# Per-engine instruction orders from a readiness planner in two attentions

## The reference

```python
s_s = jnp.einsum('bgrqd,bgqkd->bgrqk', qb, ks).astype(jnp.float32) - slopes * d_s
p_s = _masked_softmax(s_s, d_s >= 0)
o_s = jnp.einsum('bgrqk,bgqkd->bgrqd', p_s.astype(vs.dtype), vs)
...
kv = (_rmsnorm(c_kv, kv_norm) @ w_ukv).reshape(B, S, H, MLA_NOPE + MLA_V)
k_nope, v = kv[..., :MLA_NOPE], kv[..., MLA_NOPE:]
s = (jnp.einsum('bqhd,bkhd->bhqk', qn, k_nope)
     + jnp.einsum('bqhd,bkd->bhqk', qr, k_rope)).astype(jnp.float32)
p = _masked_softmax(s, kpos[None, :] <= tq[:, None])
return jnp.einsum('bhqk,bkhd->bqhd', p.astype(v.dtype), v)
```

## Time and profile before

| | |
|---|---|
| median of 3 runs | 1872.5 us (1850.19 to 1872.74) |
| profiled execution | 1867.99 us, its span 1866.4 us |
| PE matmul busy | 1539.8 us, 83% of the span |
| PE weight loads | 1231.9 us, 66% |
| DVE / ACT / POOL busy | 766.0 / 635.1 / 487.1 us |
| mean granted clock of PE | 0.887 |

### The profile page before, as it was taken

The page is one execution under the profiler, slowest core; times in us unless marked ns, Lnnn a source line. Parts: engine busy times, 40 slices in busy tenths (PEclk is TensorE's granted clock), DMA queues, the critical chain, the costliest instruction groups (busy, mean ns, idle before and its releaser), DMA issues. The chain is left out here.

```text
span 1866.4 us, 21535 instructions
## 1 busy us (share of the span) xinstructions
PE 1539.8 (83%) x8024; PEld 1231.9 (66%) x8024; DVE 766.0 (41%) x1416; ACT 635.1 (34%) x1402; POOL 487.1 (26%) x455
## 2 busy tenths in 40 slices
PE   8999997886647777877598799768889888988596
PEld 6888885554535565656477588646777777766475
DVE  2110012443565666666435000245555455555443
ACT  3112212431125556555211122225454444445200
POOL 2222221001023222221234322132243323340235
PEclk9999997656758899999799799869999999999798
DMA  5111310112031000000532222010000000000422
GB/s 169 46 51 57 123 34 21 34 34 74 1 66 40 17 18 18 18 12 1 182 102 91 74 90 83 17 54 15 15 1 15 15 15 10 6 1 1 182 102 102
DMA packets 38790, 93.51 MB, mean 50 GB/s; under 512 B 5137, under 2 KB 9250, under 8 KB 37922
## 3 DMA queue, kind: packets, MB, share of 16 engines
q1 hardware_dynamic: 38690, 92.16, 15.6%
HBM read 68.03 MB, written 18.87 MB: 47 GB/s over the span
## 5 line engine op out<-in xcount | busy, mean ns | idle before, releaser
L1092 ACT ACTIVATE mla_probs_t_hi<-mla_ps_turned 128x512 fp32r<-128x512 f32 x192 | 91.7, 490 | 156.7 <-PE mla_ps_turned L1050 155.9
L1110 DVE TENSOR_TENSOR mla_probs_t_lo<-mla_ps_turned,mla_probs_t_hi 128x512 fp32r<-128x512 f32 x192 | 105.0, 554 | 86.5 <-ACT mla_probs_t_hi L1092 85.1
L1110 DVE TENSOR_TENSOR nsa_probs_t_lo<-nsa_ps_turned,nsa_probs_t_hi 128x512 fp32r<-128x512 f32 (+1 forms) x192 | 98.7, 521 | 76.2 <-ACT nsa_probs_t_hi L1092 75.1
L237 POOL TENSOR_TENSOR l0p_w_lo<-l0p_w_raw,l0p_w_hi 128x512 fp32r<-128x512 f32 (+1 forms) x56 | 68.6, 1225 | 216.3 <-ACT l0p_w_hi L221 216.3
L1084 ACT ACTIVATE nsap_probs<-nsa_ps_scores,nsa_neg_max 128x640 f32<-128x640 f32 (+7 forms) x128 | 89.6, 700 | 71.0 <-DVE nsa_neg_max L1104 64.3
L1092 ACT ACTIVATE nsa_probs_t_hi<-nsa_ps_turned 128x512 fp32r<-128x512 f32 (+1 forms) x192 | 84.1, 461 | 82.0 <-PE nsa_ps_turned L1050 81.3
L1104 DVE TENSOR_REDUCE mla_neg_max<-mla_ps_scores 128x1 f32<-128x512 f32 (+7 forms) x128 | 96.7, 756 | 34.9 <-PE mla_ps_scores L1919 34.6
L1084 ACT ACTIVATE base_region<-mla_ps_scores,mla_neg_max 128x512 f32<-128x512 f32 (+7 forms) x128 | 94.9, 741 | 46.9 <-DVE mla_neg_max L1104 40.3
L221 ACT ACTIVATE l0p_w_hi<-l0p_w_raw 128x512 fp32r<-128x512 f32 (+1 forms) x56 | 34.0, 606 | 225.0 <-PE l0p_ps_acc L64 203.3
L1104 DVE TENSOR_REDUCE nsa_neg_max<-nsa_ps_scores 128x1 f32<-128x640 f32 (+7 forms) x128 | 90.1, 704 | 38.7 <-PE nsa_ps_scores L1303 37.8
L62 PE MATMUL out_ps_y<-out_w_hi,out_o_t_hi 128*128 128x512 f32 x256 | 104.0, 406 | 0.1
(11 more groups left out here) (255 smaller groups left out, 3941.8 us busy)
## 6 DMA issues: line engine op xcount, KB each, us to landing
l0p_w_raw<-in_w_dram SPq DMA_DIRECT2D x48, 256.0 KB, 2.7
out_w_raw<-in_w_out_dram SPq DMA_DIRECT2D x16, 512.0 KB, 4.4
l1p_w_raw<-in_w_dram SPq DMA_DIRECT2D x24, 256.0 KB, 3.1
mla_w_raw<-in_w_heads_dram SPq DMA_DIRECT2D x8, 640.0 KB, 3.8
l0p_x_raw<-in_x_t_dram SPq DMA_DIRECT2D x8, 512.0 KB, 3.4
silu_gates_scratch<-l0p_silu_out SPq DMA_DIRECT2D x16, 256.0 KB, 2.1
out_res<-in_x_dram SPq DMA_DIRECT2D x8, 512.0 KB, 5.0
x_scratch<-out_w_raw SPq DMA_DIRECT2D x8, 512.0 KB, 2.9
```

The source lines that it names most:

```text
L237: nc.gpsimd.tensor_tensor(wl[:, k % WR, 0:w], raw[:, k % RAW, 0:w], wh[:, k % WR, 0:w].bitcast(F32), ALU.subtract).then_inc(lo_ready, 1)
L1092: self.nc.scalar.activation(self.pth[:, m % N_SPLIT, c], self.p_t[f.turn_slot[m] % N_TURN][:, c], ACT.Copy).then_inc(self.hi_done, 1)
L1110: self.nc.vector.tensor_tensor(self.ptl[:, m % N_SPLIT, c], self.p_t[f.turn_slot[m] % N_TURN][:, c], self.pth[:, m % N_SPLIT, c].bitcast(F ...
```

## The change

`Flow` goes. `Plan` takes lanes: lists of tasks for one engine or a choice of engines, each task with a cost and the tasks that it needs. It repeatedly places, at the earliest possible start, the head of a lane that was ready first, and keeps an order for each engine alone. A finished task counts as seen by others REACH later (PE 200 ns, ACT and DVE 45, POOL 80). Values, backs, turns, and rows with units are four lanes of PE; evictions may go to ACT or DVE in both attentions. Turn banks are given out in the order in which turns and backs are placed.

`packed` puts several narrow key blocks of a step into one turn bank, up to four tiles: a step of the first half has 3 packs instead of 4 key blocks, one of the second half 7 instead of 8 (causal) or 5 instead of 8 (window). A pack has one `hi` and one `lo`; its transposes and value matmuls are as many as before. A turn waits for the last row that it reads, no longer for the last of the step.

In MLA the values of two pairs are projected together in even pairs, 24 matmuls of 256 columns per half, into a ring of V_SLOTS = 3 pair slots. Weight blocks are 1536 columns for even pairs, of which odd pairs load and split only 1024. All units of the next pair now alternate with the last rows of a pair; in the first pair the first row stands behind one q and one k unit. POOL waits for the previous pair's last rows before it overwrites q and k. The cost functions of the planner are `matmul_cost` max(107, 5 + 0.45 n), `act_cost` 165 + 0.845 n, `exp_cost` 455 + 0.84 n, `dve_cost` 150 + 1.055 n (ns, n columns).

```diff
+class Plan:
+
+
+
+
+    REACH = {"PE": 200, "ACT": 45, "DVE": 45, "POOL": 80, "SP": 0}
+
+    def __init__(self, n_turn):
+        self.n_turn = n_turn
+        self.lanes, self.done, self.order = [], {}, {e: [] for e in self.REACH}
+        self.slot, self.slots, self.drains = {}, [], []
+
+    def lane(self, engines, tasks, takes_slot=False):
+        self.lanes.append((engines, list(tasks), takes_slot))
+
+    def drain_lane(self, engine, drain_of):
+
+        self.lanes.append(((engine,), self.drains, False))
+        self.drain_of = drain_of
+
+    def _ready(self, tasks, takes_slot):
+        key, cost, needs = tasks[0]
+        times = [self.done.get(k) for k in needs]
+        if takes_slot and len(self.slots) >= self.n_turn:
+            times.append(self.done.get(self.drain_of(self.slots[-self.n_turn])[0]))
+        return None if None in times else max(times, default=0)
+
+    def run(self):
+        free = dict.fromkeys(self.REACH, 0)
+        while True:
+            best = None
+            for e in free:
+                heads = []
+                for n, (engines, tasks, takes_slot) in enumerate(self.lanes):
+                    if e in engines and tasks:
+                        ready = self._ready(tasks, takes_slot)
+                        if ready is not None:
+                            heads.append((ready, n))
+                if heads:
+                    ready, n = min(heads)
+                    start = max(ready, free[e])
+                    if best is None or start < best[0]:
+                        best = (start, e, n)
+            if best is None:
+                break
+            start, e, n = best
+            engines, tasks, takes_slot = self.lanes[n]
+            key, cost, needs = tasks.pop(0)
+            free[e] = start + cost
+            self.done[key] = start + cost + self.REACH[e]
+            self.order[e].append(key)
+            if takes_slot:
+                self.slot[key] = len(self.slots)
+                self.slots.append(key)
+                self.drains.append(self.drain_of(key))
+        assert not any(tasks for _, tasks, _ in self.lanes)
...
+def packed(groups):
+
+    left, packs = list(groups), []
+    while left:
+        pack = [left.pop(0)]
+        for g in sorted(left, key=lambda g: -len(g[1])):
+            if sum(len(tiles) for b, tiles in pack) + len(g[1]) <= 4:
+                pack.append(g)
+                left.remove(g)
+        packs.append(pack)
+    return packs
...
+    def seen_by(self, m):
+
+        s, pack = self.packs[m]
+        tiles = {i for b, ts in pack for i in ts}
+        return max(k for k in range(self.first_row[s], self.last_row(s) + 1) if self.steps[s]["rows"][self.rows[k][1]][0] in tiles)
...
+        plan.lane(("PE",), [(("values", m), 30 + sum(2 * matmul_cost(len(tiles) * P) for b, tiles in self.packs[m][1]),
+                             [("lo", m)] + value_needs(self.packs[m][0])
+                             + [("evict", s - 1) for s in steps if s and m == self.first_pack[s]]) for m in packs])
+        plan.lane(("PE",), [(("back", s), 428, [("evict", s)]) for s in steps], takes_slot=True)
+        plan.lane(("PE",), [(("turn", m), 107 * self.pack_cols(m) // P, [("exp", self.seen_by(m))]) for m in packs], takes_slot=True)
+        plan.lane(("PE",), main)
+        plan.lane(("ACT",), [(("exp", k), exp_cost(self.row_cols(k)), [("max", k)]
+                              + [("turn", self.last_pack(s - 2)) for s in [self.rows[k][0]] if s >= 2]
+                              + [("totals", s - 4) for s in [self.rows[k][0]] if s >= 4]) for k in range(len(self.rows))])
+        plan.lane(("ACT",), [(("hi", m), act_cost(self.pack_cols(m)), [("turn", m)] + [("values", m - N_SPLIT)] * (m >= N_SPLIT))
+                             for m in packs])
+        plan.lane(("DVE",), [(("max", k), dve_cost(self.row_cols(k)), [("row", k)]) for k in range(len(self.rows))])
+        plan.drain_lane("DVE", lambda key: (("lo", key[1]), dve_cost(self.pack_cols(key[1])), [("hi", key[1])])
+                        if key[0] == "turn" else
+                        (("totals", key[1]), 850, [("back", key[1])] + [("out", key[1] - 2)] * (key[1] >= 2)))
+        plan.lane(("ACT", "DVE"), [(("evict", s), 640, [("values", self.last_pack(s))] + [("back", s - 2)] * (s >= 2)) for s in steps])
+        plan.lane(("POOL",), [(("out", s), out_cost, [("totals", s)]) for s in steps])
...
+    later = range(2, HEADS)
+    head_end = lambda h: [("row", sm.last_row(4 * h + 3))]
+    plan.lane(("ACT",), [(("q_hi", h), 1055, head_end(h - 2)) for h in later])
+    plan.lane(("POOL",), [(("q_lo", h), 2350, [("q_hi", h)]) for h in later])
+    plan.lane(("POOL",), [(("q_bias", h), 2120, head_end(h - 2)) for h in later])
+    plan.lane(("SP",), [(("q_spread", h), 2500, [("q_lo", h)]) for h in later])
+    plan.run()
...
+        def projections(m):
+            kinds = [("q", 0, 0), ("k", 0, 0), ("k", 0, 1), ("q", 0, 1), ("v", 0, 0), ("v", 0, 1), ("q", 1, 0), ("q", 1, 1)]
+            return [("unit", (m,) + kind) for kind in kinds if kind[0] != "v" or m % 2 == 0]
+
+        if n == 0:
+            first = projections(0)
+            main += first[:2]
+            rows[1:1] = first[2:4]
+            rows[4:4] = first[4:6]
+            rows[10:10] = first[6:]
         if n + 1 < NP:
-            phases[-2].insert(1, ("weights", n + 1))
-            phases[-1].insert(1, ("unit", n + 1, "q", 0, 0))
-            phases[-1].insert(3, ("unit", n + 1, "q", 0, 1))
-    flow = Flow(steps, phases, 9)
-    sm = Softmax(core, sp, "mla", flow, p_area)
+            coming = projections(n + 1)
+            for back, x in enumerate(reversed(coming)):
+                rows.insert(len(rows) - 2 * back, x)
+        main += rows
...
+    def split_width(n):
+
+        return WW if n % 2 == 0 else WQK
...
+    plan.lane(("SP",), [(("w_load", n), 4000, [("w_lo", n - 1)] * (n > 0)) for n in pairs])
+    plan.lane(("ACT",), [(("w_hi", n), split_width(n), [("w_load", n)] + [("unit", last_unit(n - 1)) for n in [n] if n]) for n in pairs])
+    plan.lane(("POOL",), [(("w_lo", n), 2.3 * split_width(n), [("w_hi", n)]) for n in pairs])
+    plan.lane(("DVE",), [(("q_rotated", (n, h, c)), 690, [("unit", unit_at[n, "q", h, c])]
+                          + [("q_split", (x[0],) + x[2:]) for x in q_units[max(0, m - 2):max(0, m - 1)]])
+                         for m, (n, _, h, c) in enumerate(q_units)])
+    plan.lane(("POOL",), [(("q_split", (n, h, c)), 1990, [("q_rotated", (n, h, c))]
+                           + [("row", sm.last_row(4 * (n - 1) + 2 * h + c)) for n in [n] if n]) for n, _, h, c in q_units])
+    plan.lane(("ACT",), [(("k_out", (n, c)), 600, [("unit", unit_at[n, "k", 0, c])] + [("k_split", (n - 1, 1, c))] * (n > 0))
+                         for n, _, _, c in k_units])
+    plan.lane(("POOL",), [(("k_split", (n, h, c)), 1980, [("k_out", (n, c))]
+                           + [("row", sm.last_row(4 * (n - 1) + 2 * h + 1)) for n in [n] if n])
+                          for n in pairs for h in range(2) for c in range(2)])
+    plan.lane(("ACT",), [(("v_hi", (n, c)), 1200, [("unit", unit_at[n, "v", 0, c])]
+                          + [("values", sm.last_pack(4 * (n + 1 - V_SLOTS) + 3)) for n in [n] if n + 1 >= V_SLOTS])
+                         for n, _, _, c in v_units])
+    plan.lane(("DVE",), [(("v_lo", (n, c)), 1380, [("v_hi", (n, c))]) for n, _, _, c in v_units])
+    plan.run()
...
-                if kind == "q" and h == 0 and c == 0:
-                    pe.wait_ge(w_lo, n + 1)
+                pe.wait_ge(w_lo, n + 1)
                 sm.wait_bank(pe, ("unit", u), unit_drained)
                 if kind == "v":
                     for t in range(4):
                         tok = slice((4 * c + t) * P, (4 * c + t + 1) * P)
                         for k in range(KVT):
-                            col = WUQ + WUK + k * P
-                            last = mm3(pe, ps[:, 0, t * P:(t + 1) * P], (ck[0][:, k, tok], ck[1][:, k, tok]),
-                                       (wh[:, col:col + P], wl[:, col:col + P]), k == 0, k == KVT - 1)
+                            col = WQK + k * 2 * P
+                            last = mm3(pe, ps[:, t // 2, (t % 2) * 2 * P:(t % 2 + 1) * 2 * P], (ck[0][:, k, tok], ck[1][:, k, tok]),
+                                       (wh[:, col:col + 2 * P], wl[:, col:col + 2 * P]), k == 0, k == KVT - 1)
...
+                if n:
+                    pool.wait_ge(sm.scores_ready, sm.last_row(4 * (n - 1) + 2 * h + c) + 1)
...
+                if n:
+                    pool.wait_ge(sm.scores_ready, sm.last_row(4 * (n - 1) + 2 * h + 1) + 1)
...
+                ps = sm.scores_of(("unit", u))[:, :, :].rearrange("p a (b s h d) -> p (a b) s h d", b=2, s=2, h=2)
+                for k in range(2):
+                    if n + k >= V_SLOTS:
+                        act.wait_ge(sm.values_done, sm.first_pack[4 * (n + k - V_SLOTS) + 4])
```

(1 more changed line is left out.)

581 lines of the change are left out of this document (268 added, 313 removed).

## The result

The changed kernel takes 1693.36 us (median of 4 runs, 1693.28 to 1698.23) against 1862.14 us of the kernel before in the same comparison (4 runs, 1850.19 to 1872.74): a ratio of 0.9102, interval 0.9025 to 0.9178. The profiled execution took 1698.23 us (span 1696.6, mean clock 0.905) where that of before took 1867.99. The forecast was 1770 us, its range 1722 to 1825.

What follows compares the result with a forecast made beforehand. PE was taken as the bound, idling for evictions and then slowed by a low clock. The terms -72 - 25 - 19 - 3 + 4 + 20 = -95 took 1868 to 1773; forecast 1770 us, range 1722 to 1825.

Steps and rivals of the forecast that it cites:

- Backs and evictions: Step ends of both attentions: of 81 us that PE's turning back waits for evictions, 72 us go.
- The first rival: Both attentions: half of the 81 us come back as waits for banks; centre 1808 us, chance 0.19.
- Granted clock: Both attentions: of 55 us of withheld full clock, 25 us come back as gaps go; bounds 0 and 38.
- two discounts: Clock term: 80% of 47 us counted as falling on busy PE time, 38 us; two thirds of that taken, 25.
- Value pairs: Second attention: 384 value matmuls of 128 columns become 192 of 256, 19 us less PE time.
- the bound of 8 us for the banks: Second attention, value projections: 8 longer holds of score banks could each stall the rows 1 us more.
- Packs: Both attentions: 80 fewer copies on ACT and 80 fewer subtractions on DVE, mostly hidden by PE; 3 us less.
- Start: Start of the second attention: PE idles some 3 us for POOL's splits, wider first weights add 1 us; +4 us.
- New waits: PE meets not-ready results more often: 12 us in the first attention, 8 in the second; +20, bounds 0 and 60.
- The rival called deeper: Both attentions: all idle time but starts and ends, and all withheld clock, go; -149 us, 1719 us, chance 0.15.
- The rival of the score banks: Both attentions: the two score banks become the bound as maxima and exponentials queue; slower, 1917 us, chance 0.06.
- the 85 that I had named: First attention: the forecast called itself wrong if DVE is busy over 85% of it.

Runs made afterwards that it cites:

- e9: Kernel before, first attention only: ACT's eviction put ahead of the last high-part copy and last exponential issued before it, PE's order untouched; ratio 0.983.
- e2: Kernel before, with the turning back of a step's result put on PE three events behind the last values instead of one; ratio 0.9998.
- e13: Kernel before, with evictions moved ahead as in e9, but in both attentions and on DVE as well as ACT; ratio 0.9558.
- e6: Changed kernel with values projected for one pair at a time again, 16 units of 128 columns; ratio 0.9211.
- e5: Changed kernel without packs, each key block in a turn bank of its own; ratio 0.9181.
- e12: Changed kernel with the old start of the second attention, both q and both k units ahead of the first row; 1689.9 us, ratio 0.9095.
- e10: Changed kernel with PE's and POOL's planned orders, but ACT and DVE walking PE's list by the old rules; ratio 0.9387.
- e14: Changed kernel with ACT alone walking PE's order by the old rules, DVE and POOL as planned, each eviction keeping its engine; ratio 0.933.
- e15: Changed kernel with DVE alone walking PE's order by the old rules, ACT and POOL as planned; ratio 0.9285.
- e7: Changed kernel whose planner, among tasks that could start at the same moment, takes the first lane instead of the one ready first; ratio 0.9289.
- e11: Changed kernel edited as in e10, with the back also planned at the step's last values, not after the eviction; 1770.3 us, ratio 0.954.
- e1: Kernel before, with ACT evicting the accumulator at the event of the last values, not at the one after; ratio 0.9807.
- e3: Kernel before with the edits of e1 and e2 together; ratio 0.987.

## Why the prediction was wrong

The bound was read rightly: PE, its waits for evictions, and the clock. The sum failed on two terms: the clock's was too small, and that of the new waits had the wrong sign. A part of PE's busy time that goes with each wait had no term at all.

*Backs and evictions, -72.* 81.2 us became 4.6 (2.8 of the back, 1.8 of values): -77. Right, and e9 shows that it is order and not space: with the same accumulator and PE's order kept, ACT's 37.0 became 2.2. The first rival (1808 us, the gaps move) falls with it; its mechanism is what e2 shows.

*Granted clock, -25, bounds 0 and 38: mis-sized, and its upper bound too low.* I had 55 us withheld, from rounded means (28.8 + 22.9 = 51.7 us by the trace), and gave 8 to the starts. That much was right: over 4-us windows that leave out the first 8 to 12 us of each stretch, the withheld clock was 24.8 and 20.5 us before and is 0.6 and 0.7 after. The two discounts were wrong. 80% for low clock in idle time assumed that it is spread like the work. But laid over PE's busy intervals in the trace, 26.8 of the 28.8 us and all 22.9 fall on busy time, so the low clock lies behind the gaps and not in them; the earlier trace rows could have told, with a slow window that was busy for 3.73 of its 4 us. Two thirds assumed that a third of the falls would stay. On busy time 4.1 and 4.7 us are left, so the term was -41 where I had -25.

*Ends of matmuls before a wait: no term.* PE's busy time fell by 27 us in the first attention and by 46.4 - 19.6 = 27 in the second with the same work, 13 us more than the 41 of the clock. An estimate accounts for it: a matmul of 0.27 us in a stream is followed by the next after 0.11, but one before a wait is counted to its end, 0.16 us more. PE waited 132 times in the two attentions before (the starts left out) and 61 times after, and 71 x 0.16 = 11 us. e9 and e13 are the counter-check in the first attention. The clock on busy time fell by 22.5 and 22.7 us there, the waits rose from 65 to 81, by the estimate 3 us; so 20 us of busy time should go, and 17 and 15 went. So the account holds to some 3 to 5 us, and a part of the clock's 41 can be of other origin.

*Value pairs, -19.* PE's busy time says -19.6, and three starts lie 0.36 us apart as reckoned:

```profile
1175.18 0.28 PE L62 MATMUL mla_ps_scores<-mla_w_hi,l1b_ckv_hi 128*128 128x256 f32 x1
...
1175.54 0.28 PE L62 MATMUL mla_ps_scores<-mla_w_hi,l1b_ckv_hi 128*128 128x256 f32 x1
```

The stage says -14.8, for the waits that e6 shows; the bound of 8 us for the banks was ample for the 5 that came.

*Packs, -3.* e5: -2.6. *Start, +4.* e12: +3.6 (2.2 us of it waits, the rest busy time, at a clock that differs by 0.004), and the row stands where it was expected, behind POOL's splits:

```profile
1166.43 1.25 POOL L1975 TENSOR_TENSOR l1b_k_lo<-mla_k_nope,l1b_k_hi 64x512 fp32r<-64x512 f32 x1
...
1167.79 0.60 PE L62 MATMUL mla_ps_scores<-l1b_k_hi,mla_q_hi 128*128 128x512 f32 x1 [2.73 <-issue]
```

*New waits, +20: the wrong sign.* The step that failed is "hi, lo, maximum and exponential follow each other more tightly; PE will meet a not-ready result more often than now". For an eviction that is only moved ahead, it holds: e13 has 17 us of it. But in the change the other waits of PE fell from 42.5 us to 26.3 (those at the starts and the 2.7 of the first row left out): -16 where +20 stood. It isn't the orders of ACT and DVE that took them away: with these undone the same waits are 17.6 us in e10 and 18.4 in e14, and 28.3 in e15. Where PE stands waiting for evictions, other results get ready in the meantime, so a part of that is hidden and not gone. With the rule of the planner changed (e7), where evictions hold PE up for no more than 2.9 us, they are 42.4 us, as before. So what avoids the small waits is the planned order by readiness, as far as these runs show PE's own, while the orders of ACT and DVE mainly avoid the waits for evictions. I had costed the planner through the one wait that I could see in a row, and took the small, spread ones as a floor.

The sum by what was measured, in waits of PE and in its busy time: -77 of evictions, -16 of other waits and +3 at the start, then -20 of pairs, -41 of clock and -11 of ends before waits, -162 in all for the two attentions, where the windows say -163. The packs' 3 us and the 5 us that the pairs give back are inside the other waits. The rival called deeper had the sign of every term and most of the sizes (15 us of other waits gone, against 16), but stopped at 38 us of clock and had no term for the ends. With 41 us of clock it would have been 1716. Its chance of 0.15 was too low because the forecast took the discounts as facts.

The rival of the score banks (1917 us) fell: PE waits 4.1 us for them in the first attention, DVE is busy 198 of 255 us (78%, under the 85 that I had named).

The experiments split the 164 us from two sides. From before: the eviction's place in the old lists 72 (e13), value pairs 15 (e6), packs 3 (e5), the start -4 (e12), and 78 that came with nothing short of the whole change. From after: ACT's and DVE's own orders 49 (e10), the back behind its eviction 23 (e11), the same 15 + 3 - 4, and again 78, which stay when only PE's planned order is left. The two sides overlap: the same gaps close by an earlier eviction or by rows and turns planned around it, so none of these numbers is the price of one part by itself. No run has PE's old order with planned orders on the others, and none has PE's planned order without the units' new places, so how the 78 split stays open. So does their exactness: the side from before carries the 15 us said above.

## What to carry to other kernels

When an engine waits for an instruction that stands late in another engine's in-order list, move that instruction in its own list before moving the one that waits: the first was worth 72 us here and the second nothing. Count the clock that repeated gaps withhold where it lies: here nearly all of it (49.7 of 51.7 us) lay on busy time behind the gaps, and 41 us came back. Count with each wait that goes the end of the matmul before it, too, by the estimate 0.16 us here. And when a hand-made order gives way to one by readiness, the small waits in the list of waits are part of what can go, not a floor.

## What the runs showed of the hardware

The granted clock answered to the gaps in a way that isn't in proportion. In e1 the waits for evictions shrank from 47.9 to 40.9 us in the first attention, and the windows of 4 us under 0.985 went from 24 of 80 to 2 of 73. In e3 they were 34.9 us, the longest 2.3, fewer and shorter than in e1, and 18 of 78 windows were under it. In e11, with 43.4 us of such waits, it was 16 of 74. In the second attention of e13 the longest wait for an eviction was 1.1 us, and 8 of 112 windows were still under 0.985, 3 of them under 0.6 (before: 19 of 119, 5). Neither the sum of the waits nor the longest alone orders these runs; which property of the gaps does, is open. Each figure is of one execution.
